# A bias line made earlier, raw weights loaded a stage ahead, and wider key blocks in a hybrid attention step

## What is computed

```python
def merge(oa, za, ob, zb, ga, gb, wa, wb, wo):
    ya = jnp.einsum('btc,cd->btd', oa * jax.nn.silu(za), wa)
    yb = jnp.einsum('btc,cd->btd', ob * jax.nn.silu(zb), wb)
    m = jax.nn.sigmoid(ga) * ya + jax.nn.sigmoid(gb) * yb
    return jnp.einsum('btd,de->bte', m, wo)
# per group: h = rmsnorm(x, norm_g)
# qa, ka, va, qi, wi, ki, za, qb, kb, vb, zb, ga, gb = split(h @ w_in)
# A: an indexer scores all keys by sum over its heads of relu(qi.ki) * wi; every query keeps the top 256
#    keys and attends to them (8 heads, 2 key heads, depth 128, a relative bias per head)
# B: attention over a window of the query's own 64-frame chunk and the two chunks before it
#    (16 heads, 2 key heads, depth 64, a learned sink per head, a relative bias per head)
# x += merge(oa, za, ob, zb, ga, gb, w_br_a, w_br_b, w_out), then a last rmsnorm; keys and values are outputs too
```

## Time and profile before

| | us |
|---|---|
| median of 3 runs (3305.42 to 3307.70) | 3307.67 |
| the profiled execution, whole | 3306.38 |
| its span in the trace | 3304.2 |

### The profile page before, as it was taken

The page is one execution under the profiler, slowest core; times in us unless marked ns, Lnnn a source line. Parts: engine busy times, 40 slices in busy tenths (PEclk is TensorE's granted clock), DMA queues, the critical chain, the costliest instruction groups (busy, mean ns, idle before and its releaser), DMA issues. The chain is left out here.

```text
span 3304.2 us, 48487 instructions
## 1 busy us (share of the span) xinstructions
PE 3132.3 (95%) x17925; PEld 2950.9 (89%) x17925; DVE 1304.2 (39%) x2453; ACT 916.4 (28%) x1898; POOL 1032.7 (31%) x773
## 2 busy tenths in 40 slices
PE   6999999999999999889999799987989999899997
PEld 6999999999999989889999788876779999888875
DVE  5001562755667549900000266444863112120401
ACT  5111122121323131111111355434653111121422
POOL 1222211212222322222222466435752222133443
PEclk9999999999999999999999899998999999999999
DMA  4232222223232322153222553346535433253442
GB/s 159 65 81 75 75 63 73 72 67 83 71 100 74 97 75 80 52 145 95 82 80 79 153 147 103 96 108 148 128 91 173 125 104 119 84 209 105 162 137 99
DMA packets 432083, 341.55 MB, mean 103 GB/s; under 512 B 37244, under 2 KB 391644, under 8 KB 428428
## 3 DMA queue, kind: packets, MB, share of 16 engines
q1 hardware_dynamic: 398992, 275.97, 30.3%
q10 hardware_dynamic: 32956, 63.77, 6.0%
HBM read 264.25 MB, written 75.48 MB: 103 GB/s over the span
## 5 line engine op out<-in xcount | busy, mean ns | idle before, releaser
L466 POOL TENSOR_TENSOR w_in_tile_lo<-w_in_tile_raw,w_in_tile_hi 128x512 fp32r<-128x512 f32 x316 | 410.4, 1300 | 1393.7 <-ACT w_in_tile_hi L486 1393.7
L594 PE MATMUL banks<-h_early_hi,w_in_tile_hi 128*128 128x384 f32 x2496 | 639.9, 337 | 3.8 <-POOL w_in_tile_lo L466 3.8
L594 PE MATMUL banks<-h_early_hi,w_in_tile_lo 128*128 128x384 f32 x2496 | 636.6, 336 | 0.0
L594 PE MATMUL banks<-h_early_lo,w_in_tile_hi 128*128 128x384 f32 x2496 | 636.1, 336 | 0.0
L486 ACT CAST w_in_tile_hi<-w_in_tile_raw 128x512 fp32r<-128x512 f32 x316 | 196.2, 621 | 1254.1 <-PE banks L594 1127.8
L594 PEld LDWEIGHTS banks<-h_early_hi,w_in_tile_hi 128*128 128x128 f32 x2496 | 434.8, 188 | 13.0 <-issue 5.1
L594 PEld LDWEIGHTS banks<-h_early_hi,w_in_tile_lo 128*128 128x128 f32 x2496 | 434.8, 188 | 0.0
L594 PEld LDWEIGHTS banks<-h_early_lo,w_in_tile_hi 128*128 128x128 f32 x2496 | 434.7, 188 | 0.0
L761 DVE MAX8 top<-score 128x8 f32<-128x384 f32 (+6 forms) x224 | 247.2, 1103 | 33.0 <-DVE score L764 1.1
L2319 POOL TENSOR_TENSOR w_out_tile_lo<-w_out_tile_raw,w_out_tile_hi 128x512 fp32r<-128x512 f32 x128 | 175.7, 1377 | 222.7 <-ACT w_out_tile_hi L2329 222.7
L764 DVE MATCH_REPLACE8 score<-top,score 128x384 f32<-128x384 f32 (+6 forms) x224 | 243.0, 1085 | 0.0
(11 more groups left out here) (244 smaller groups left out, 4970.0 us busy)
## 6 DMA issues: line engine op xcount, KB each, us to landing
w_in_tile_raw<-in_w_in SPq DMA_DIRECT2D x440, 256.0 KB, 2.9
w_out_tile_raw<-in_w_out SPq DMA_DIRECT2D x128, 256.0 KB, 3.1
product<-spill ACTq DMA_DIRECT2D x46, 544.0 KB, 3.3
u_b<-product SPq DMA_DIRECT2D x32, 544.0 KB, 6.4
product<-spill ACTq DMA_DIRECT2D x32, 384.0 KB, 2.5
merged<-u_b ACTq DMA_DIRECT2D x16, 544.0 KB, 7.4
x_rows<-in_x_prompt SPq DMA_DIRECT2D x8, 1024.0 KB, 5.0
b_q_raw<-product SPq DMA_DIRECT2D x32, 256.0 KB, 4.7
```

The source lines that it names most:

```text
L466: pool.tensor_tensor(s.w_lo[:, q, :, :], s.w_raw[:, q, :, :], s.w_hi[:, q, :, :].bitcast(F32), ALU.subtract).then_inc(lo_made, 1)
L594: last = pe.matmul(ps[0:m, 3 * slot + c, 0:w], w_[:, q, kq, 0:m], tokens, start=(k == 0 and w_ is s.w_hi and h_ is s.h_hi), stop=(k == KT ...
```

## The change

The mark "bias line" goes to a place behind the second tile of the group that precedes score block 2: PE's product, DVE's copy and ACT's broadcast are made there, and the constants are loaded at "prompt keys". The rest of the old mark (mask, rolls, loading the sample's keys and values) stays as "load the sample", one tile later than before. DVE waits for the broadcast before the sample's scores.

Each stage gets the two first late tiles of the next stage. `project` loads both of `attend_prompt`'s; in a stage the loads begin with the third tile (index 8), and a new `load_rest` loads the last quarter of the next stage's second tile and waits until its quarters have landed.

In `attend_b` the second key block has 128 rows: `prob` is 256 wide with zeros behind column 192, and the missing value rows are zeroed, by two memsets on POOL; the values' splits are merged. The query casts of unit n + 4 (`Q_RING`) stand where those of n + 3 stood, and unit 3's are made before the loop.

```diff
@@ -269,22 +269,22 @@
 
-def project(nc, s, w_in, cache_kidx, rel_bias, one_hot, cache_b_k, cache_b_v, outs, late_tile):
+def project(nc, s, w_in, cache_kidx, rel_bias, one_hot, cache_b_k, cache_b_v, outs, late_tiles):
 
...
     plan = [(QI, 2, "copy", None), "natural", (QI + 2 * P, 6, "copy", None), "prompt keys",
-            (QA, 2, "copy", None), (QA + 2 * P, 1, "copy", 2), (QA + 3 * P, 3, "copy", None),
+            (QA, 2, "copy", None), "bias line", (QA + 2 * P, 1, "copy", 2), (QA + 3 * P, 3, "copy", None),
             (QA + 6 * P, 1, "copy", 3), (QA + 7 * P, 4, "copy", None), (QA + 11 * P, 1, "copy", 4), (QB, 4, "copy", None),
...
             ("sample keys", 2),
-            (GA + 20 * P, 2, "early", NB), (QB + 9 * P, 1, "copy", None), (GA + 22 * P, 8, "early", None),
-            "bias line", (GA + 30 * P, 2, "early", None),
+            (GA + 20 * P, 2, "early", NB), (QB + 9 * P, 1, "copy", None), (GA + 22 * P, 9, "early", None),
+            "load the sample", (GA + 31 * P, 1, "early", None),
             "turn the sample", (ZA, NB, "silu", None), (ZB, NB, "silu", None)]
@@ -416,6 +416,8 @@
                 elif what == "prompt keys":
+                    sp.dma_start(table, rel_bias).then_inc(consts_in, 16)
+                    sp.dma_start(hot, one_hot).then_inc(consts_in, 16)
                     sp.wait_ge(nat_copied, 3)
@@ -440,11 +442,8 @@
                     uses += 1
-                elif what == "bias line":
+                elif what == "load the sample":
                     store_mask(NB)
-                    sp.dma_start(table, rel_bias).then_inc(consts_in, 16)
-                    sp.dma_start(hot, one_hot).then_inc(consts_in, 16)
-
                     sp.dma_start(outs["s_b_k"][0, 0, 0:CHUNK], cache_b_k[0, 0, CHUNK:WINDOW]).then_inc(rolled, 16)
@@ -455,7 +454,10 @@
                     load_queries(x)
-            load_tile(n_tiles, 0, 0, late_tile)
+            for k in range(2):
+                load_tile(n_tiles + k, 0, 0, late_tiles[k])
+            for q in range(QUARTERS):
+                sp.wait_ge(w_in_q[q], 16 * (n_tiles + 1))
             sp.wait_ge(rolled, 32)
@@ -544,10 +546,12 @@
                         act.wait_ge(kv_stored, 16 * (SAMPLE_STORES + BLOCK_STORES * NB + 2))
-                        act.wait_ge(line_stored, 16)
                     else:
...
                 elif what == "bias line":
+                    act.wait_ge(line_out, 1)
+                    act.dma_start(s.lines[:], line.unsqueeze(1).to_broadcast([H_A + H_B, P, RELS])).then_inc(line_stored, 16)
+                elif what == "load the sample":
                     act.wait_ge(mask_made, len(blocks))
@@ -560,8 +564,6 @@
                     act.dma_start(s.v_b[SEQ:T, :], kv_nat[0:DEC, 5 * P:6 * P]).then_inc(kv_stored, 16)
-                    act.wait_ge(line_out, 1)
-                    act.dma_start(s.lines[:], line.unsqueeze(1).to_broadcast([H_A + H_B, P, RELS])).then_inc(line_stored, 16)
             act.wait_ge(spilled[0], 16 * ((n_tiles + 1) // 2))
@@ -619,6 +621,7 @@
                     pe.wait_ge(consts_in, 32)
+                    pe.wait_ge(nat_copied, 3)
                     pe.matmul(ps[0:H_A + H_B, 7, 0:RELS], table, hot, start=True, stop=True).then_inc(line_done, 1)
@@ -727,6 +730,8 @@
                                 dve.wait_ge(mask_made, blocks.index(b))
+                            if k == 0 and b == NB:
+                                dve.wait_ge(line_stored, 16)
                             dve.tensor_scalar(score[:, c:c + w], ps[:, 6 + n % 2, 0:w], weights(h), None,
@@ -769,7 +774,8 @@
                     dve.tensor_copy(line, ps[0:H_A + H_B, 7, 0:RELS]).then_inc(line_out, 1)
-                    dve.wait_ge(line_out, 1)
+                elif what == "load the sample":
+                    dve.wait_ge(mask_made, len(blocks))
                     dve.sem_inc(kv_copied, 1)
@@ -803,6 +809,7 @@
         self.tiles = len(columns)
+        self.split = QUARTERS * (self.tiles + (1 if following else 0))
         assert self.steps_before[-1] == self.tiles * KT and max(points) <= 12 and min(points) >= 0
@@ -810,34 +817,44 @@
 
-    def quarters(self, p, ahead):
-
-        return range(*(min(4 * len(self.columns), self.steps_before[x] // 4 + ahead) if x >= 0 else QUARTERS for x in (p - 1, p)))
+    def quarters(self, p, ahead, ready, end):
+
+        return range(*(max(ready, min(end, self.steps_before[x] // 4 + ahead)) if x >= 0 else ready for x in (p - 1, p)))
+
+    def load_quarter(self, sp, n):
+        t, q = divmod(n, QUARTERS)
+        sp.wait_ge(self.w_lo_made, n - 7)
+        src = self.w_in[0, q * KQ * P:(q + 1) * KQ * P, self.columns[t]:self.columns[t] + P]
+        sp.dma_start(self.s.w_raw[:, q, :, :], src.rearrange("(k p) c -> p k c", p=P)).then_inc(self.w_loaded[q], 16)
 
     def load(self, sp, p):
-        for n in self.quarters(p, 7):
-            t, q = divmod(n, QUARTERS)
-            if t > 1:
-                sp.wait_ge(self.w_lo_made, n - 7)
-            src = self.w_in[0, q * KQ * P:(q + 1) * KQ * P, self.columns[t]:self.columns[t] + P]
-            sp.dma_start(self.s.w_raw[:, q, :, :], src.rearrange("(k p) c -> p k c", p=P)).then_inc(self.w_loaded[q], 16)
+        for n in self.quarters(p, 7, 2 * QUARTERS, QUARTERS * len(self.columns)):
+            self.load_quarter(sp, n)
+
+    def load_rest(self, sp):
+        end = QUARTERS * len(self.columns)
+        for n in range(min(end, self.steps_before[-1] // 4 + 7), end):
+            self.load_quarter(sp, n)
+        for q in range(QUARTERS):
+            sp.wait_ge(self.w_loaded[q], 16 * (len(self.columns) - 2))
 
     def split_hi(self, act, p):
-        for n in self.quarters(p, 4):
+        for n in self.quarters(p, 4, QUARTERS, self.split):
             t, q = divmod(n, QUARTERS)
             act.wait_ge(self.w_used, n - 3)
-            act.wait_ge(self.w_loaded[q], 16 * t)
+            if t > 1:
+                act.wait_ge(self.w_loaded[q], 16 * (t - 1))
             act.copy(self.s.w_hi[:, q, :, :], self.s.w_raw[:, q, :, :]).then_inc(self.w_hi_made, 1)
...
     def split_lo(self, pool, p):
-        for n in self.quarters(p, 4):
+        for n in self.quarters(p, 4, QUARTERS, self.split):
             q = n % QUARTERS
...
     def splits_done(self, pool, p):
-        made = self.quarters(p, 4).stop - QUARTERS
+        made = self.quarters(p, 4, QUARTERS, self.split).stop - QUARTERS
         if made:
@@ -1030,6 +1047,7 @@
                 gates.load(sp, p)
+            gates.load_rest(sp)
             for g in range(groups - 2, groups):
@@ -1658,10 +1677,10 @@
         if b == NB:
-            return W_S, [(CACHED, P, 0), (OWN, CHUNK, P)]
+            return W_S, [(CACHED, P, 0), (OWN, P, P)]
         if b == 0:
             return (half + 1) * CHUNK, [(0, (half + 1) * CHUNK, 0)]
-        return W_S, [(half * ODD + b - 1, P, 0), (half * ODD + b, CHUNK, P)]
+        return W_S, [(half * ODD + b - 1, P, 0), (half * ODD + b, P, P)]
 
@@ -1688,7 +1707,7 @@
         q_pair = sb("q_stacked", [P, Q_RING, HEADS, CHUNK], F32R)
-        prob = sb("prob", [P, RING, PAIRS, W_S])
+        prob = sb("prob", [P, RING, PAIRS, NEAR])
         small = sb("small", [P, RING, 5, PAIRS])
@@ -1779,13 +1799,11 @@
                 if part == 0:
-                    rows = [(slice(0, P), slice(0, NB))]
+                    tiles = slice(0, NB)
                 else:
-                    rows = [(slice(0, CHUNK), slice(OWN - 1, OWN + 1)), (slice(0, P), slice(CACHED, CACHED + 1)),
-                            (slice(0, P), slice(ODD, OWN - 1))]
-                for r, tiles in rows:
-                    last = pool.tensor_tensor(v_lo[r, tiles, :], v_raw[r, tiles, :], v_hi[r, tiles, :].bitcast(F32), ALU.subtract)
-                last.then_inc(v_made, 1)
+                    tiles = slice(NB, CACHED + 1)
+                pool.tensor_tensor(v_lo[:, tiles, :], v_raw[:, tiles, :], v_hi[:, tiles, :].bitcast(F32), ALU.subtract).then_inc(
+                    v_made, 1)
 
@@ -1794,12 +1812,17 @@
 
+            pool.memset(prob[:, :, :, W_S:NEAR], 0.0).then_inc(padded, 1)
+            pool.wait_ge(padded, 1)
+            pool.memset(v_raw[CHUNK:P, OWN - 1:OWN + 1, :], 0.0).then_inc(padded, 1)
+            pool.wait_ge(padded, 2)
             q_lo_of(0)
...
             q_lo_of(2)
+            q_lo_of(3)
             values_lo(0)
@@ -1808,10 +1831,10 @@
                 gates.split_lo(pool, START + n)
-                if n + 3 < len(units):
+                if n + Q_RING < len(units):
                     pool.wait_ge(p_made, n + 2)
                     gates.splits_done(pool, START + n)
-                    q_lo_of(n + 3)
+                    q_lo_of(n + Q_RING)
             gates.split_lo(pool, START + len(units))
@@ -1856,9 +1879,8 @@
                     act.wait_ge(v_in[1], 64)
-                    act.copy(v_hi[0:CHUNK, OWN - 1:OWN + 1, :], v_raw[0:CHUNK, OWN - 1:OWN + 1, :])
-                    act.copy(v_hi[:, CACHED, :], v_raw[:, CACHED, :])
```

(18 more changed lines are left out.)

## The result

The changed kernel takes 3320.44 us in the median of six runs (3315.99 to 3323.07), the kernel before 3306.55 in the same comparison (six runs, 3303.93 to 3308.76). The ratio is 1.0038 with a 95% interval of 1.0029 to 1.0048: slower by 0.38%, which is clear of 0.2%. The forecast was 3306, no change, with a range up to 3316. The profiled execution of the changed kernel took 3319.11 us, its span 3317.3 (3304.2 before).

What follows compares the result with a forecast made beforehand. TensorE, busy 95% of the span, bounds the kernel, so only its stalls or slow running count. +18.0 - 12.5 + 4.6 - 1.6 + 2.5 - 0.6 - 10 = +0.4 us against 3306.38: 3306, own range 3298 to 3314, with rivals 3288 to 3316.

Steps and rivals of the forecast that it cites:

- B's start: Start of attend_b: about 6 us of PE's 8.99 us wait go, a query wait eats 4; gain 2 us.
- Part 1a: Late in the projection: PE's waits of 16.60 and 3.76 us give way to one of 4.4; gain 18.0 us.
- Part 1b: Ahead of score block 2: the early bias line delays query casts, PE idles 10.2 us, half clock follows; cost 12.5 us.
- Part 2, prompt and sample: Raw weights loaded a stage early: prompt +4.6 at start, -1.6 at end; sample +2.5 at start, -0.6 at end.
- The prompt's start: Start of attend_prompt: PE's 6.60 us wait for its second tile's last quarter shrinks to some 3 us; gain 4.6 us.
- The sample's 2.5 us: Start of attend_sample: PE's 3.27 us mask wait shortens because three weight loads ahead on SP go; gain 2.5 us.
- The ends of the stages: SP waits for the following tile's last quarter before the last stores; cost 1.6 us in prompt, 0.6 in sample.
- Part 3, the three stalls: attend_b, units 10, 20 and near the end: DVE's query casts wait for late loads; 4.2 us each, 12 in all.
- Plain units: attend_b's other units: DVE 1.6 us late every second unit, PE's 0.3 us saving not had; 0 for the pace.
- rival 3: attend_b's query loop sets the pace, waits over 2 us in every even unit, another 7 to 10 us: 3315; chance 0.15.
- B in all: attend_b: +2 at the start, 0 in plain units, -12 for stalls, together -10 us; bounds +2 and -17.
- Rival 4: Late tiles' early loads only move the collision, yielding nothing, and new stage-end waits stay: 3312; chance 0.10.

Runs made afterwards that it cites:

- 3297.82: The changed kernel with attend_b as in the kernel before (64-row blocks, queries cast three units ahead): 3297.82 us, ratio 0.9974.
- part 2 alone: The kernel before with only the two following late tiles, loads from the third tile on and stage-end waits for the last quarter: 3300.66 us, ratio 0.9979.
- the experiment: The changed kernel with the bias line's mark ahead of the two tiles instead of behind them: 3304.87 us, ratio 0.9994.
- the kernel with the queries first: The changed kernel with SP issuing raw query loads ahead of late weights in each step of B's loop: 3281.38 us, ratio 0.9926.
- the last one: The changed kernel with bias line and query loads both moved ahead, stage-end wait behind the stores, B's last queries loaded a step sooner: 3267.35 us, ratio 0.9873.

## Why the prediction was wrong, point by point

By runs, the parts of the change are: part 1, 3297.82 - 3300.66, a gain of about 3 us; part 2 alone, a gain of 5.8; part 3, a loss of 22.6. Each is the difference of two neighbouring kernels, so that they add to the 13.9 us between the medians proves nothing more. Parts 1 and 2 with B's start were forecast at +12.4 and gave 9.2; part 3 was forecast at -12.

The waits forecast are there in the trace, at the places and with the releasers named, except that the sample's wait for its mask stayed in this execution. What failed are the sizes of three terms. Forecast and trace differ by 13.5 us: 7.4 in the prompt and the sample, 5.0 in B and 1.8 at the early line, less 0.7 over all other places. Term by term:

- **Part 1a, +18.0:** right, 18.1 by the traces, with the rest of the wait at 4.42 us (4.4).
- **Part 1b, -12.5:** the mechanism right, the size short: 14.3 by the traces, 15.6 by the experiment. The step that failed is that the weights would be no later than the queries. Their way from issue to PE was taken from the earlier trace rows as 5.3 us; here it took 6.9, and with it the wait ended. ACT began to cast the first quarter 4.5 us after the issue, 3.2 us after that of the earlier trace rows in the kernel before; here the second pair of query loads was issued just ahead of it. That this pair is the cause is not shown.
- **Part 2, prompt and sample, +4.9 in all:** the largest miss in this trace. From attend_prompt's first matmul to attend_b's it takes 379.7 us, 377.2 before: 2.5 lost. The prompt's start gained 3.5 and 3.1 went to half clock behind waits of 1.4 us, which no step of the prediction held. That this is the clock and not the order of work is seen in the kernel with the queries first, whose stretch after the same two waits is

```profile
1873.20:1878.20 5.00, 4.97 (x36) 1.00 0.60 150
```

  with the time between the two events of the table 29.9 us as before, not 33.0; five other kernels with the same prompt took 31.7 to 31.8, and the last one 33.0. Why the clock falls in one execution and not in the next was not settled. The sample's 2.5 us was absent from this execution, where the wait for the mask was 3.78 us; in the seven other kernels with part 2 that wait is gone. The ends of the stages cost 2.2 and 1.0 us (1.6 and 0.6 forecast), and the end of the projection, which now waits for two tiles, 0.6, which had no term. In those seven the whole stretch gained 0.1 to 4.4 us, so the forecast was too high for all of them, and a loss is seen in this execution alone.
- **B's start, +2:** 6.5 us of the wait went (8.99 to 2.51 us), 6 forecast. What the queries take back there was sized 4 us and was 5.9, so that 0.7 was left at the turn of unit 10.
- **Part 3, the three stalls, 4.2 each:** by the runs the term with the largest miss. The turns of units 10 and 11, and of 20 and 21, are 12.60 and 13.39 us apart where they were 6.88 and 6.80, so the two stalls cost 5.7 and 6.6; the third cost 5.6: 17.9 and not 12. I had reckoned DVE's lateness of 6.9 us nearly rightly (7.25, 7.87) and taken from it what PE would not feel. PE's waits grew from 1.33 to 6.24 us and from 1.26 to 7.03, by 4.9 and 5.8 where 4.2 was forecast, and I had not added the half clock behind a wait of that length, though I counted it twice in the projection. 15 instructions in 4 us where 28 are usual is some 1.8 us for each.
- **Plain units, 0:** right. With DVE's cast waiting about 2 us in even units, units 11 to 20 took 51.3 us, before 51.2: PE's saving and DVE's wait cancel. The sign of rival 3, waits of over 2 us in every even unit, is nearly there (1.8 to 2.4 us in most), but its loss of pace is not.
- **B in all, -10:** -15.0 by the traces. The bound of -17 allowed it; the range ended at 3316 because the other terms were expected to miss to both sides. Here they missed to one side, and in the prompt and in B for the same reason: a wait was priced without the clock behind it. Rival 4, that part 2 yields nothing, fits the prompt and the sample of this one execution, but not part 2 alone, which gained 5.8 us.

The Trainium skill ("TensorE: Matmul & The Clock Gate", section "LDWEIGHTS (loading the stationary operand)") has a weight load's time independent of its rows, and the trace agrees, with 0.18 and 0.19 us. The prediction took steps between matmuls for load times when it said that the trace differs, and from equal loads it does not follow that padding gains nothing: the rows differ in when the load starts. The estimate of 2.6 us for a load of 256 KB, by the Trainium skill ("DMA: Bandwidth & Descriptors", section "Anatomy of one DMA — SWDGE (gpsimd) path"), does not hold for these loads, with a median of 4.6 us before and after. That section's formula is for DMAs issued from GpSimd, and SP issues these, so no run here tests it.

## What to carry to other kernels

When a consumer is moved one step sooner, move the load that feeds it by the same step, and look at what stands ahead of that load in its queue: here the order of two lines on the issuing engine was worth 39 us, once the casts had been moved. An instruction inserted into an in-order queue is priced by what is behind it, including the transfers that another engine issues only after it. And a wait on TensorE can cost more than its length: the waits of 10.78, 6.24 and 7.03 us here were each followed by some 4 us at a granted clock of 0.50 to 0.56. Add both to every stall in a sum, not only to the one where it was noticed.

## What the runs showed that I had not expected

Casting the queries four units ahead, with its loads on time, is worth 10 us over three units ahead (3281.38 against 3291.34), though waits for queries were only 5.1 us in B's long loop. The traces place it, 11.3 us in B: 7.2 are had by the turn of unit 4, ahead of the loop that I had looked at, 7.9 between units 4 and 29, and 3.7 are given back where the last unit's cast waits for its load. And two waits of 1.4 us in the prompt are followed by full clock in one execution and by 0.50 for 5 us in another, with 0 to 3 us between them.
